# The first weights piece and the second piece of x issued from ScalarE's DMA queue instead of SyncE's

## The reference, cut to what matters

```python
h = rms_norm(x, norm_w[l], NORM_EPS)
proj = h @ w_in[l]                       # 256 x 2048 by 2048 x 7704
(q_a, kc_a, vc_a, ks_a, vs_a, kw_a, vw_a, g_a, z_a,
 q_b, k_b, v_b, z_b) = jnp.split(proj, split_points, axis=-1)
o_a = nsa_mixer(...)                     # compressed, selected and window branches
o_b = diff_mixer(...)                    # two softmax maps
mixed = jnp.concatenate([o_a * jax.nn.silu(z_a), o_b * jax.nn.silu(z_b)], axis=-1)
x = x + mixed @ w_out[l]
```

## Time and profile before

| | |
|---|---|
| time, median of 3 runs | 487.11 us (486.92 to 487.83) |
| the profiled execution's own time | 487.29 us |
| its span, first to last instruction | 485.5 us |
| PE busy | 476.0 us, 98% |
| DVE, ACT, POOL busy | 355.6, 233.5, 45.8 us |
| read from HBM | 105.20 MB |

### The profile page before, as it was taken

The page is one execution under the profiler, slowest core; times in us unless marked ns, Lnnn a source line. Parts: engine busy times, 40 slices in busy tenths (PEclk is TensorE's granted clock), DMA queues, the critical chain, the costliest instruction groups (busy, mean ns, idle before and its releaser), DMA issues.

```text
span 485.5 us, 6561 instructions
## 1 busy us (share of the span) xinstructions
PE 476.0 (98%) x2574; PEld 388.8 (80%) x2574; DVE 355.6 (73%) x477; ACT 233.5 (48%) x336; POOL 45.8 (9%) x49
## 2 busy tenths in 40 slices
PE   8999999999999999999999999999999999999994
PEld 7888868686868888878888888888888888888883
DVE  5855996468778798998978656588897998454533
ACT  6747424233334465846546455554436443534331
POOL 1003400020202002020200000102000000303050
PEclk9999999999999999999999999999999999999998
DMA  8999999887945425144453524445775355654004
GB/s 282 416 419 415 415 416 361 336 321 323 361 173 196 168 95 186 80 169 173 174 173 98 174 98 180 157 173 216 279 284 188 159 189 197 242 218 193 1 0 174
DMA packets 18734, 107.71 MB, mean 222 GB/s; under 512 B 2320, under 2 KB 2960, under 8 KB 7440
## 3 DMA queue, kind: packets, MB, share of 16 engines
q1 hardware_dynamic: 17264, 104.34, 56.5%
q10 hardware_dynamic: 1440, 2.96, 1.6%
HBM read 105.20 MB, written 2.10 MB: 221 GB/s over the span
## 4 chain that ended last, share of the span: by engine, by line
PE 92%; DVE 4%; issue 1%; DMA 1%; ACT 1%; POOLq 0%; SPq 0%; DVEq 0%; POOL 0%; ACTq 0%
PE acc L1191 25%; PE acc L1193 25%; PE acc L1192 25%; PE O L1250 3%; PE acc L1230 1%; PE acc L1233 1%; PE acc L1237 1%; DVE kbT L850 1%; PE S L1367 1%; PE S L1382 1%; DVE wlo L786 1%; DMA raw<-head 1%; PE O L1416 1%; PE S L1355 0%; PE O L1405 0%
## 5 line engine op out<-in xcount | busy, mean ns | idle before, releaser
L786 DVE TENSOR_TENSOR wlo<-raw,whi 128x2048 fp32r<-128x2048 f32 x71 | 164.4, 2317 | 84.7 <-ACT whi L487 84.2
L487 ACT ACTIVATE whi<-raw 128x2048 fp32r<-128x2048 f32 x71 | 136.0, 1917 | 140.5 <-PE acc L1193 130.1
L1191 PE MATMUL acc<-whi,hT_hi 128*128 128x512 f32 x432 | 170.1, 394 | 0.6 <-DVE stage L841 0.6
L1193 PE MATMUL acc<-whi,hT_lo 128*128 128x512 f32 x432 | 168.3, 390 | 0.0
L1192 PE MATMUL acc<-wlo,hT_hi 128*128 128x512 f32 x432 | 168.2, 389 | 0.0
L1191 PEld LDWEIGHTS acc<-whi,hT_hi 128*128 128x128 f32 x432 | 81.1, 188 | 20.7 <-issue 3.4
L1193 PEld LDWEIGHTS acc<-whi,hT_lo 128*128 128x128 f32 x432 | 81.1, 188 | 17.0
L1192 PEld LDWEIGHTS acc<-wlo,hT_hi 128*128 128x128 f32 x432 | 81.2, 188 | 16.5
L437 POOL TENSOR_TENSOR stage<-stage,stage 128x512 f32<-128x512 f32 (+1 forms) x16 | 23.4, 1481 | 174.8 <-DVE stage L841 174.8
L582 ACT ACTIVATE e<-S,small 128x128 f32<-128x128 f32 (+1 forms) x48 | 19.5, 419 | 21.4 <-DVE small L899 21.4
L850 DVE STREAM_TRANSPOSE zT<-stage 32x256 f32<-32x256 f32 x64 | 27.9, 435 | 2.0
(11 more groups left out here) (202 smaller groups left out, 534.9 us busy)
## 6 DMA issues: line engine op xcount, KB each, us to landing
raw<-stream SPq DMA_DIRECT2D x71, 1024.0 KB, 4.8
row_raw<-stream SPq DMA_DIRECT2D x8, 1024.0 KB, 7.5
row_x<-stream SPq DMA_DIRECT2D x4, 1024.0 KB, 9.9
raw<-head SPq DMA_DIRECT2D x6, 512.0 KB, 8.1
raw<-head SPq DMA_DIRECT2D x8, 256.0 KB, 4.8
x_nat<-x_rows SPq DMA_DIRECT2D x2, 1024.0 KB, 14.9
row_x<-stream SPq DMA_DIRECT2D x4, 512.0 KB, 10.7
row<-stream SPq DMA_DIRECT2D x4, 512.0 KB, 11.7
```

The source lines that it names most:

```text
L487: act.activation(whi[:, n % SPLIT, :], raw[:, n % RAW, :], ACT.Copy).then_inc(hi_ready, 1)
L786: dve.tensor_tensor(wlo[:, n % SPLIT, :], raw[:, n % RAW, :], whi[:, n % SPLIT, :].bitcast(f32), ALU.subtract)\
L1191: pe.matmul(acc_bank(n), xh, wh, start=k == 0, stop=False)
L1193: last = pe.matmul(acc_bank(n), xl, wh, start=False, stop=k == KT - 1)
```

## The change

Two DMAs move from SP's program to ACT's: w0 and x1. In ACT's program they stand behind the DMA of `nw` and ahead of the table load. Sizes, sources, destinations, semaphores and the layout of `head` stay as they are.

```diff
@@ -91,6 +91,7 @@
+ON_ACT = [("w", 0), ("x", 1)]
 HEAD_CHUNKS = 5
@@ -357,6 +358,8 @@
             for kind, i in FIRST[:-1]:
+                if (kind, i) in ON_ACT:
+                    continue
                 if kind == "x":
                     x_piece(sp, i)
                 else:
@@ -476,6 +479,8 @@
             act.dma_start(nw[:, :], norm_w).then_inc(nw_in, 16)
+            act.dma_start(raw[:, 0, 0:NB], head_piece(ON_ACT[0])).then_inc(w_in[0], 16)
+            x_piece(act, ON_ACT[1][1])
             act.wait_ge(warm_ready, 1)
             act.activation(small[:, 60:61], warm[:, 0:1], ACT.Copy)
```

## The result

The change makes the kernel slower: 489.87 us (median of 6 runs, 487.65 to 489.94) against 487.18 us (6 runs, 486.92 to 487.83), a ratio of 1.0040 with a 95% interval of 1.0030 to 1.0049. (The ratio weighs all runs and is not the quotient of the medians, which is 1.0055; the two differ where the runs fall into two groups.) The forecast was 487.3 us, no change. The runs of the change lie apart: four at 489.9, one at 488.45, one at 487.65 us. The profiled execution took 489.89 us, 2.60 us more than the profiled one of before.

What follows compares the result with a forecast made beforehand. PE was taken to bound the kernel, with a reachable hole of 0.665 us. w0's later landing gave +0.28 us, 487.39 us on the median, lowered to 487.3 us for a possible gain; range 486.4 to 488.2 us.

Steps and rivals of the forecast that it cites:

- What bounds the kernel, and the hole: PE bounds the kernel; its only reachable idle time, before the second group (w1), is worth 0.665 us.
- The ceiling of the gain: At PE's start, no better arrival of the pieces can gain more than 0.67 us, below the measurable 0.97 us.
- ACT's two issues: On ACT, 0.46 us each; table load at 2.09 us, the 0.92 us delay covered by waits except 0.07 us.
- w0's landing: On ACT's queue, packets alternate with w1's; landing at 4.8 instead of 3.86 us, third group +0.28 us.
- the price of the two groups behind the idle stretch: PE's first two groups, taken at full pace: 1.45 + 1.365 us after a first matmul at 5.44 us.
- rival 4: PE's clock falls during the longer wait after warm-up; four groups at half pace cost 5.5 us, 492.8 us; chance 0.01.
- Rival 1: At PE's start, w0 lands as now, w1 at 5.25 us or sooner; 486.4 to 486.7 us; chance 0.25.
- Rival 3: At ACT's wait for w0, w0 is starved, landing after 5.5 us; 488.3 or 489.5 us; chance 0.14.
- The range: Whole kernel: 486.4 to 488.2 us, leaving out a w0 landing past 5.6 us and the clock.
- The last step: Whole-kernel sum: 487.39 us lowered to 487.3 us because the landing's middle is coarse and a gain leans the other way.

Runs made afterwards that it cites:

- the two small DMAs: Kernel before, with two 8 KB position-table DMAs issued by ScalarE behind norm_w's, ahead of the table load; 487.57 us against 487.19, ratio 1.0008.
- The second measurement: The changed kernel unaltered, run again on another occasion against the kernel before; 488.04 us (12 runs) against 487.37, ratio 1.0018.

## Why the prediction was wrong, step by step

- **What bounds the kernel, and the hole:** right. Nothing moved behind the third group, and the hole behind the first group closed. The ceiling of the gain was not put to the test, since no order tried gained anything.
- **ACT's two issues:** right in size (table load at 2.13 us, forecast 2.09) and in being covered (the two small DMAs).
- **w0's landing:** the direction was right, and sharing with w1 is part of the cause; the term was sized at 4.8 us and measured 5.1 us. The part that was missing is that w0 hardly flowed before 3.2 us, the cause of which stays open. First matmul 5.70 us instead of 5.44, change from it +0.54 us instead of +0.28. With this alone the kernel would be at 487.18 + 0.54 = 487.7 us; 10 of its 18 runs lie between 487.4 and 488.5 us.
- **The failed step is the price of the two groups behind the idle stretch.** The sum adds them at the full pace, 1.45 + 1.365 = 2.815 us; they took 10.61 - 5.70 = 4.91 us. What should have guarded it is rival 4, "The granted clock falls while PE waits longer between warm-up and first group", with a chance of 0.01. It came near the mechanism and was thrown out by a column, and by a wait in the wrong place: the 0.41 us that it names stand ahead of the second group, behind six real matmuls, and between warm-up and first group there was no wait before. The warm-up of the earlier trace rows runs at 3.45/40 = 0.086 us for 104 columns, which is the 1.2 GHz level, while PEclk says 1.00. In all 14 profiled executions the warm-up begins at this pace. So nothing falls: the rise comes late. The price given, 5.5 us for four groups, was too high; it is 2.09 us for ten matmuls here. The Trainium skill, "TensorE: Matmul & The Clock Gate", Part 1, says that "the default state is throttled, and activity releases the throttle"; the warm-up's pace agrees.
- **Rival 1** (landing follows issue) fell: w0 did not keep its 3.86 us. w1 landed at 4.9 us, but it did so in one execution without the change too. The Trainium skill, "DMA: Bandwidth & Descriptors", under "Issuing engines are not separate DMA queues", says that issuing from a second engine only saves the sequencer's issue time. By that w0 would have landed as before; it landed 1.2 us later, and the measurement decides.
- **Rival 3** (w0 starved, landing past 5.5 us) was not what happened, though its total of 488.3 to 489.5 us comes near. **The range** ended at 488.2 us because the clock was priced as all but excluded. The second measurement's median of 488.04 us lies inside it, by the luck of eight fast starts in twelve, and not because the mechanism was right. **The last step** of the sum, from 487.39 down to 487.3 us for the case of a gain, went the wrong way.

That the slow group of the changed kernel's runs is the late rise of the clock is shown in both profiled executions of it (489.89 and 489.71 us); for runs without a profile it is inferred from their time.

## What to carry to other kernels

A DMA moved to a second queue is not ahead of what the first queue holds: once both flowed, they moved equal parts (0.18 MB each from 3.2 to 4.2 us). Where the first group needs three inputs, bringing one forward held another back in three of the orders tried here (w0 ahead of `norm_w`, x0 alone on ACT, `norm_w` on SP). Read TensorE's level at a program's start from the pace of equal matmuls, not from the granted share. Whatever delays the first matmul behind a warm-up has to be priced with the clock on top; where the first input may be late, try a longer warm-up (56 instead of 40 matmuls took most of the loss away here, and 46 cost the kernel before nothing).

## What the runs showed of the hardware

- The level rose at different moments in executions of nearly the same start: within the 40 warm-up matmuls of the kernel before (they took 3.45 us, against 3.65 us where all are slow), not within 56 of them in another (5.03 us of unbroken work), and in the changed kernel after the tenth real matmul, past 10 us. In eight of the 14 profiled executions the slow pace was over by 7 us, in the other six it lasted until 9.0 to 10.3 us, and in none did it end between. All six late ones had PE idle for 0.71 us or more ahead of the first real matmul, among them the changed kernel and the one with 26 matmuls. Of the eight early ones seven had at most 0.61 us of it, and one had 0.92 us (`norm_w` on SP). So the idle stretch makes a late rise likely and doesn't settle it; what does is not shown.
- 8 KB in rows of 64 bytes, second in a queue beside 256 KB pieces, took 3.8 us from issue to landing; first in its queue beside x0 it took 2.2 to 2.4 us.
- The kernel before has the late rise too, seldom: in a set of 29 runs one took 489.76 us and the others 486.75 to 488.07, and in a set of 17 one took 489.46 us; in the other sets, 54 runs, none was above 488.3 us. That those two were the late rise is inferred from their time.
